# Decay rows of a state-space step: a 1 MB spread from memory, or 8 KB and a GpSimd broadcast

## What is computed

```
for l in range(2):
    proj = rms_norm(x) @ w_in[l]
    y_ssd = ssd_branch(z, xbc, dt, ...)        # conv of 5 taps, SiLU, state-space sums in both directions
    y_att = attention_branch(q, k, v, bias)    # 24 heads, windows of dilation 1, 4, 16
    x = x + (sig(gA)*(y_ssd @ w_ssd_out) + sig(gB)*(y_att @ w_attn_out)) @ w_out
    x = x + peer_ffn(rms_norm(x))              # 8 heads x top 16 of 16384 experts for each token
return rms_norm(x)
```

## Time and profile before

| | us |
|---|---|
| median of 3 runs | 4048.46 (4048.27 to 4052.55) |
| span of the profiled execution | 5878.7 |
| PE busy in it | 5726.4 (97%) |
| DVE busy | 2887.4 (49%) |
| ACT busy | 1648.5 (28%) |
| POOL busy | 1285.3 (22%) |
| moved by DMA | 1444.45 MB |

### The profile page before, as it was taken

How to read it: one execution, slowest core, us unless ns; L and a number is a source line. 1 busy time by engine, 2 the same in 40 slices (tenths; PEclk the granted TensorE clock), 3 DMA queues, 4 the chain that set the end, 5 groups by cost and what they waited for, 6 DMA issues and landing times.

```text
span 5878.7 us, 40315 instructions
## 1 busy us (share of the span) xinstructions
PE 5726.4 (97%) x13374; PEld 2787.7 (47%) x13374; DVE 2887.4 (49%) x5745; ACT 1648.5 (28%) x4216; POOL 1285.3 (22%) x1094
## 2 busy tenths in 40 slices
PE   9999999999999998999999999899999999899999
PEld 5555555444444545444445545344445555222222
DVE  3321003665555455756555555756555554744443
ACT  3431101344422211244432211245422211222222
POOL 0000000222222221322222221322222221334343
PEclk6555555555555555555555555555555555555555
DMA  4222222767777775767777775777777775899997
GB/s 155 93 102 81 73 90 95 267 238 266 261 275 268 274 280 202 285 245 280 273 272 297 283 291 190 280 256 271 271 268 308 281 290 191 315 350 342 345 342 281
DMA packets 212948, 1444.45 MB, mean 246 GB/s; under 512 B 27256, under 2 KB 27256, under 8 KB 46340
## 3 DMA queue, kind: packets, MB, share of 16 engines
q0 software_dynamic: 164976, 1133.94, 52.0%
q1 hardware_dynamic: 47632, 307.80, 14.4%
q10 hardware_dynamic: 132, 0.12, 0.0%
HBM read 1439.31 MB, written 7.13 MB: 246 GB/s over the span
## 4 chain that ended last, share of the span: by engine, by line
PE 96%; DVE 2%; ACT 1%; issue 1%; DMA 0%; SPq 0%; ACTq 0%; DVEq 0%
PE banks L609 52%; PE sums L871 21%; PE banks L871 7%; PE banks L748 5%; PE banks L827 3%; PE banks L669 2%; PE banks L736 1%; PE banks L786 1%; PE banks L778 1%; PE banks L694 1%; PE banks L844 1%; DVE x L1479 1%; DVE rows L1470 0%; PE banks L637 0%; PE banks L700 0%
## 5 line engine op out<-in xcount | busy, mean ns | idle before, releaser
L609 PE MATMUL banks<-hT,ring 128*128 128x256 f32 x6656 | 2608.4, 583 | 4.7 <-DVE arena L1316 3.9
L609 PEld LDWEIGHTS banks<-hT,ring 128*128 128x128 f32 x6656 | 1507.5, 228 | 1151.7 <-issue 734.0
L576 POOL DMA_INDIRECT rows<-in_w_uv,idx x1024 | 1237.6, 1209 | 3600.3 <-PE sums L871 1981.3
L1470 DVE CUSTOM_DVE_ANT_0 rows<-rows,xn 128x1024 f32<-128x1024 f32 x1024 | 1241.6, 1220 | 530.8 <-DMA rows<-in_w_uv,idx 528.0
L871 PE MATMUL sums<-rows,diag 128*128 128x512 f32 x1612 | 1285.2, 970 | 70.0 <-ACT diag L1076 47.9
L1479 DVE SCALAR_TENSOR_TENSOR x<-rows,wgt,x 128x1024 f32<-128x1024 f32 x493 | 632.0, 1282 | 234.8 <-ACT wgt L1068 234.0
L871 PEld LDWEIGHTS sums<-rows,diag 128*128 128x128 f32 x1612 | 369.2, 232 | 791.7 <-issue 683.2
L1281 DVE SCALAR_TENSOR_TENSOR arena<-banks,pr,arena 128x254 f32<-128x254 f32 (+1 forms) x512 | 246.8, 482 | 354.6 <-ACT arena L965 340.9
L1063 ACT ACTIVATE gelu<-hid 128x2 f32<-128x2 f32 x512 | 102.9, 201 | 1100.7 <-DVE hid L1470 1099.3
L609 PE MATMUL banks<-yT,ring 128*128 128x256 f32 x1024 | 400.2, 582 | 0.0
L871 PE MATMUL banks<-rows,diag 128*128 128x512 f32 x512 | 393.7, 966 | 0.0
(11 more groups left out here) (205 smaller groups left out, 2955.8 us busy)
## 6 DMA issues: line engine op xcount, KB each, us to landing
ring<-in_w_ssd SPq DMA_DIRECT2D x96, 1024.0 KB, 5.4
ring<-in_w_att SPq DMA_DIRECT2D x64, 1024.0 KB, 6.1
ring<-in_w_mrg SPq DMA_DIRECT2D x52, 1024.0 KB, 8.4
arena<-a_rows POOLq DMA_DIRECT2D x32, 1024.0 KB, 7.6
ring<-in_w_qry SPq DMA_DIRECT2D x32, 1024.0 KB, 4.8
arena<-bias_tiles POOLq DMA_DIRECT2D x16, 1152.0 KB, 7.3
ring<-in_w_out SPq DMA_DIRECT2D x16, 1024.0 KB, 7.0
rows<-in_w_uv,idx POOLq DMA_INDIRECT x1024, 6.8
```

What stands on the lines that cost most here:

```text
L576: nc.gpsimd.indirect_dma_start(out=rows[n % NB][:, :], out_offset=None, in_=w_uv, in_offset=bass.IndirectOffsetOnAxis(ap=idx[:, t, s:s + 1 ...
L609: mm = pe.matmul(out, w[:, k * P:(k + 1) * P], rhs[:, k0 + k, :], start=start and k == 0, stop=stop and k == n - 1)
L1470: v.tensor_tensor_reduce(u, u, xn2[:, (n // SLOTS_T) % 3, :], 1.0, 0.0, ALU.mult, ALU.add, hid[:, k:k + 1]).then_inc(u_done, 1)
```

## The change

The DMA of `decay_rows` writes only partition 0 of `aBC` (8 KB). A new `broadcast_rows(g)` waits on POOL for that transfer (`dr_in`) and then has GpSimd copy partition 0 of `aBC` to all 128 partitions, in place. It stands at 0.75 of group 0 and at 0.55 of each later group. By the table of ticks 2 gathers stand between the transfer and the broadcast in passes 1 to 3, and 1 for group 0 of each pass and for groups 4 and 7 of passes 2 and 3. `mask(g)` waits for the broadcast in place of the DMA.

```
         aBC = cut(2, RH, SEQ)
+        aBC_rows = aBC.rearrange("p d h t -> p (d h t)")
...
-        aT_out, bc_in = count("aT_out", 16), count("bc_in", 16 * GROUPS)
+        aT_out, dr_in, bc_in = count("aT_out", 16), count("dr_in", 16 * GROUPS), count("bc_in", GROUPS)
...
                 def decay_rows(g):
-                    src = spread(a_dram[:, g * RH:(g + 1) * RH, :].rearrange("d h t -> d (h t)"), 0, P)
-                    pool.dma_start(aBC.rearrange("p d h t -> p d (h t)"), src).then_inc(bc_in.sem, 16)
+
+                    src = a_dram[:, g * RH:(g + 1) * RH, :].rearrange("d h t -> d (h t)").unsqueeze(0)
+                    pool.dma_start(aBC[0:1].rearrange("p d h t -> p d (h t)"), src).then_inc(dr_in.sem, 16)
+
+                def broadcast_rows(g):
+
+                    pool.wait_ge(dr_in.sem, dr_in.at(m, 16 * (g + 1)))
+                    pool.partition_broadcast(aBC_rows, aBC_rows[0:1]).then_inc(bc_in.sem, 1)
...
                 decay_rows(0)
+                yield place("ssd", 0, 0.75)
+                broadcast_rows(0)
                 for g in range(1, GROUPS):
                     yield place("ssd", g, 0.4)
                     pool.wait_ge(ex.sem, ex.at(m, 4 * g))
                     decay_rows(g)
+                    yield place("ssd", g, 0.55)
+                    broadcast_rows(g)
...
-                    v.wait_ge(bc_in.sem, bc_in.at(m, 16 * (g + 1)))
+                    v.wait_ge(bc_in.sem, bc_in.at(m, g + 1))
```

## The result

The changed kernel takes 4070.63 us in the median (4065.03 to 4077.95, 4 runs), the kernel before 4049.49 us. The ratio is 1.0054, with a 95% interval of 1.0040 to 1.0068. That is 22 us slower; the forecast was 4015 us and faster.

The account below looks back on a forecast made before the run. The prediction took PE to bound pass 0 and DMA, at about 385 GB/s, the passes after. From 4048.5 us it took 33 us of returned DMA time, with thin gather cover adding 0 to 7, and said 4015 us, range 3980 to 4075.

Parts of the forecast that it names:

- what the DMA engines give when always busy: From pass 1 on, the timed kernel was taken to stand at the DMA engines, at 385 GB/s on average.
- Part 1: Decay transfers shrink from 1.05 MB to 8 KB: ceiling 65 us in passes 1 to 3, half returned, 33 us.
- Part 2: The GpSimd broadcast of 2048 columns: 2.4 us each, hidden in passes 1 to 3; without cover 58 us.
- what hides it is the queue of gathers already issued: Gathers already queued were to cover the broadcast in passes 1 to 3; without that cover it would cost 58 us.
- GpSimd and DVE hold each other: Rival: DVE stands still for each broadcast, 58 us more in passes 1 to 3, time 4073 us; chance 0.07.
- The sign named against it: DVE's dot staying at 1.22 us would show no lock between GpSimd and DVE.
- DVE's gaps: Argument against DVE being held in ssd: gaps in DVE's work would absorb the broadcasts; no size given.
- Part 3: POOL's wait for the 8 KB, landing in 6.8 us: 0 us with two gathers queued, about 7 us in all with one.
- The first rival: POOL is held at the broadcast waiting for the 8 KB, gathers issue late, 91 us less 65: 4074 us; chance 0.16.
- Hidden anyway: Rival: DVE's order or PE sets the ssd stage, DMA time was slack: 4048 us within 8; chance 0.17.
- The whole ceiling: Rival: all 65 us of DMA time saved in passes 1 to 3 come back, 3983 us; chance 0.06.
- The dear broadcast: Rival: each broadcast takes the upper bound, 12.2 us, costing 192 us less 65: 4175 us; chance 0.04.

Follow-up runs that it names:

- fill: Changed kernel with a GpSimd memset of the same 128x2048 words in place of the broadcast, decay rows left out; ratio 0.9968 to the kernel before.
- 8 KB and the wait: Changed kernel without the broadcast, GpSimd's wait for the 8 KB transfer kept, 127 partitions left unfilled, exponentials with constant bias; ratio 0.9958 to the kernel before.
- two halves: Changed kernel with the broadcast in two 1024-column halves, each started after a convolution's first tap, and the small transfer issued earlier; ratio 0.9984 to the kernel before.
- beside the convolution: Changed kernel with the broadcast started after DVE's first of four convolution taps of column block 3, place 0.61 for 0.55; ratio 1.0015 to the kernel before.
- broadcast twice: Changed kernel with each broadcast done twice, the second started when the first is complete; ratio 1.0163 to the kernel before.
- 1 MB and the broadcast: Kernel before with its 1 MB transfer kept, and GpSimd's wait and broadcast added behind it; ratio 1.0093 to the kernel before.

## Why the prediction was wrong

*What bounds the timed kernel.* Right: the full clock (0.945 in the mean), pass 0 on PE, DMA next, and even the length of the ssd stage of pass 2, 365 us forecast and 365.4 measured (by luck in part: its own rate, 393, lies near the mean that was used). Wrong: "what the DMA engines give when always busy" was set at 385 GB/s. That was an average over stages at 423 to 427 (att, mrg, the end), 382 to 393 (ssd) and 349 (query to norm). A mean was taken for a ceiling, and so all stages seemed equally at it. At 427 GB/s the 140.4 MB of ssd would take 329 us, and DVE's 322 us were no longer 12% behind but level.

*Part 1, the DMA saving.* A ceiling of 65 us, half returned, 33 us. Measured: 17 us, a quarter. The mechanism is right, the size was halved once too little. In ssd DMA is one of several limits; a megabyte taken away returned 0.7 us (17 us over 24), one put in cost 1.0 us, against 2.9 in mrg, at 423 GB/s. The DMA rate of the ssd stage fell by 32 GB/s (393 to 361) at the same PE time, twice the 15 named.

*Part 2, the broadcast: the step that failed.* Its duration was right (2.4 forecast, 2.29 when not held, 2.67 in the mean). Wrong was "what hides it is the queue of gathers already issued". This looked at the gathers and GpSimd's queue only; what had to be hidden was the time in which DVE stands still. The rival "GpSimd and DVE hold each other" named it and priced it at 58 us of DVE time and at 4073 us. DVE's time grew by 39.4 us (some broadcasts fall on taps or gaps), and the kernel took 4070.63. The sign named against it, a dot that stays at 1.22 us, failed: 3.17. That 4073 and 4070.63 lie so near is luck: the rival had 58 us of cost on 33 of saving, measured were 39 and 17. I gave it 0.07, and against it I set only "DVE's gaps" - in a stage in which I had just computed DVE at 322 of 343 us. That was the misjudgment: the sentence of the Trainium skill stood there, no row spoke against it, and DVE was the nearly full engine. That this is the main cause is shown: kernels that differ in DVE's held time differ in the time in the same order, and with the fill both go. It isn't the whole where DVE's time grew in pass 0: counted in passes 1 to 3 alone, two versions took 14 and 19 us more than DVE's held time, and that stays open.

| against 8 KB and the wait | DVE us more | of it in passes 1 to 3 | time us more |
|---|---|---|---|
| fill | -0.7 | -0.4 | 4 |
| two halves | 7.3 | 7.4 | 10 |
| beside the convolution | 16.8 | 16.7 | 23 |
| changed | 40.2 | 38.2 | 39 |
| broadcast twice | 78.9 | 63.7 | 83 |
| 1 MB and the broadcast, against before | 37.6 | 23.8 | 38 |

*Part 3, the wait for the 8 KB.* Right. The landing was 7.2 us in the median (6.8 taken), 1.8 at the least. So most of the 8 KB transfers did land late, as behind the gathers, but no run here separates a queue's order from that of the semaphore writes. GpSimd waited 82.5 us in all, 26 times (3.2 us each, under the 5 named), and that cost nothing. The first rival, with 0.16, didn't happen: DVE waited 514.3 us for gathers, 517.4 in the kernel before at the same clock. DVE's waits for its decay rows fell from 43.6 us (4) to 24.9 us (3); I had said 0 to 3 us each, it was more, and without effect.

*The other rivals.* Hidden anyway: no, 17 us came back. The whole ceiling: no. The dear broadcast: no.

*The range* of 3980 to 4075 held the time, through its slow rivals; the forecast itself had the wrong sign.

*Open.* Why a fourth of the saving returns and not some other share isn't explained, only measured, nor are the 14 and 19 us beyond DVE's held time. Not tried was a way to broadcast that neither reads SBUF on GpSimd nor loads DVE.

## What to carry to other kernels

Before moving work to GpSimd, ask which DVE instructions will run beside it: in these traces a GpSimd broadcast, which reads SBUF, held the DVE instructions with two SBUF operands that it met, by up to 2 us each, and a copy with one. Where DVE is nearly full, 38 us of this in passes 1 to 3 came with 39 us of time. The moment can be chosen, with a wait that starts it beside DVE work on PSUM. Count only the passes in which DVE's time matters: what is held in another one (here pass 0) is in the page's total all the same. And a mean rate is no ceiling: take the ceiling from the stage where the rate is flat, and price a megabyte in the stage from which it is taken.

## What the runs showed that was not expected

A DMA share of 0.98 went with a rate of 393 GB/s that could still rise to 404, while at 427 GB/s the share reads 1.01: the share of busy time hardly tells a full DMA from one with room. The two profiled executions of one and the same kernel before had granted TensorE clocks of 0.555 and 0.945, and spans of 5878.7 and 4047.1 us. What bounded the one (PE, 97%) didn't bound the other (PE 84%). GpSimd's fill of 128x2048 words took 1.81 us and its broadcast 2.29 us.
